# One program for the four head groups of a layer, with common buffers and the next group's first projection ahead of the last unit's turns

## The reference

```python
for l in range(DEPTH):                      # 2 layers, the context output only in the first
    h = rms_norm(x, pre_mix_g[l]) * (1 + sc1) + sh1          # x: 512 latent tokens; hc likewise: 256 context tokens
    p = split(h @ w_in[l])                                    # one input projection for four head groups
    oa = A: 4 query and 2 key/value heads of 64, RMS norm of q and k, 2-D rotary, dense
    ob = B: 4 heads of 64 + 32 (rotary), keys and values from a normed latent of 128 @ w_kv_up
    oc = C: 4 query and 2 key/value heads, keys within 128 tokens, a sink logit per head
    od = D: 4 heads, 2-D neighbourhood, a learned bias per head and offset
    # latent queries attend to their latent keys and all context keys, context queries to context keys
    x = x + g1 * rms_norm(concat(oa, ob, oc, od) @ w_out[l], post_mix_g[l])
    x = x + g2 * rms_norm(moe(h2), post_ffn_g[l])             # 64 experts, top 8, and a shared expert
# sh1, sc1, g1, sh2, sc2, g2 = split(silu(c) @ ada_w[l] + ada_b[l])
```

## Time and profile before

| stage | from to (us) | us | TensorE busy | clock |
|---|---|---|---|---|
| layer 0, A | 52.8 to 177.0 | 124.2 | 115.47 | 0.93 |
| layer 0, B | 177.0 to 317.4 | 140.4 | 126.50 | 0.96 |
| layer 0, C | 317.4 to 433.7 | 116.3 | 103.10 | 0.97 |
| layer 0, D | 433.7 to 572.7 | 139.0 | 130.82 | 1.00 |
| layer 1, A | 1645.9 to 1750.3 | 104.4 | 96.04 | 0.93 |
| layer 1, B | 1750.3 to 1873.1 | 122.8 | 108.31 | 0.93 |
| layer 1, C | 1873.1 to 1963.1 | 90.0 | 79.78 | 1.00 |
| layer 1, D | 1963.1 to 2080.5 | 117.4 | 110.71 | 1.00 |

### The profile page before, as it was taken

One profiled execution on the slowest core, in us unless ns is written; L12 is line 12 of the kernel. 1 busy time (PEld: TensorE's weight loads), 2 busy tenths in 40 slices (PEclk: granted clock), 3 DMA queues, 4 the chain that ended last, 5 costly groups with the idle time before them and its releaser, 6 DMA issues. The chain is left out here.

```text
span 2915.5 us, 44582 instructions
## 1 busy us (share of the span) xinstructions
PE 2595.9 (89%) x13635; PEld 1267.2 (43%) x13636; DVE 1081.1 (37%) x3197; ACT 588.0 (20%) x1379; POOL 390.1 (13%) x312
## 2 busy tenths in 40 slices
PE   7999989896899999999996588989978999899894
PEld 3566555543433333333332266666533333333331
DVE  3443360515333333333332643451433332233233
ACT  2323241402011111111111341331310111111111
POOL 1000001001022222221221200001010212112212
PEclk9999999997999999999998799999989999999997
DMA  7120303007478998999993402202156999998983
GB/s 275 50 91 30 130 12 132 32 13 287 169 236 301 353 327 284 324 325 334 328 367 81 188 1 90 87 34 96 37 215 235 361 397 392 389 391 297 388 313 106
DMA packets 104979, 619.27 MB, mean 212 GB/s; under 512 B 22832, under 2 KB 23088, under 8 KB 64688
## 3 DMA queue, kind: packets, MB, share of 16 engines
q1 hardware_dynamic: 71184, 530.30, 46.2%
q0 software_dynamic: 33696, 87.63, 12.3%
HBM read 578.84 MB, written 77.99 MB: 225 GB/s over the span
## 5 line engine op out<-in xcount | busy, mean ns | idle before, releaser
L1513 PE MATMUL ps<-wgu,xT 128*64 128x512 f32 x3584 | 808.0, 604 | 43.1 <-DMA wgu<-in_exp_gu 34.2
L1513 PEld LDWEIGHTS ps<-wgu,xT 128*64 128x64 f32 x3584 | 253.8, 139 | 502.2 <-issue 492.2
L1522 PE MATMUL ps<-wd,hiddenT 128*64 128x512 f32 x1824 | 420.3, 603 | 11.2 <-issue 10.8
L624 PE MATMUL ps<-w_in,hT 128*128 128x512 f32 (+5 forms) x1152 | 369.0, 479 | 14.7 <-PEq L574 3.8
L1442 POOL DMA_INDIRECT ffn_rows<-Y,six x114 | 182.6, 1602 | 1110.8 <-issue 635.3
L1695 DVE TENSOR_TENSOR hidden<-silu,ps 128x256 f32<-128x256 f32 x112 | 47.2, 421 | 704.3 <-ACT silu L1631 698.5
L624 PEld LDWEIGHTS ps<-w_in,hT 128*128 128x128 f32 x1152 | 218.0, 196 | 155.7 <-issue 136.0
L1522 PEld LDWEIGHTS ps<-wd,hiddenT 128*64 128x64 f32 x1824 | 123.2, 137 | 227.7 <-issue 227.7
L1631 ACT ACTIVATE silu<-ps 128x256 f32<-128x256 f32 x112 | 43.1, 385 | 797.7 <-PE ps L1513 797.7
L1626 ACT ACTIVATE Y<-ps,wc 128x512 f32<-128x512 f32 x114 | 78.4, 688 | 417.4 <-PE ps L1522 417.4
L1689 DVE TENSOR_SCALAR Y<-ps,wc 128x512 f32<-128x512 f32 x114 | 85.6, 751 | 198.4 <-PE ps L1522 198.4
(11 more groups left out here) (490 smaller groups left out, 2724.1 us busy)
## 6 DMA issues: line engine op xcount, KB each, us to landing
wgu<-in_exp_gu SPq DMA_DIRECT2D x128, 2048.0 KB, 22.9
wd<-in_exp_d SPq DMA_DIRECT2D x128, 1024.0 KB, 8.2
ada_start<-in_ada_w SPq DMA_DIRECT2D x8, 1024.0 KB, 8.0
w_in<-in_w_in SPq DMA_DIRECT2D x4, 2048.0 KB, 10.8
w_in<-in_w_out SPq DMA_DIRECT2D x4, 2048.0 KB, 12.4
aw_0A<-in_ada_w SPq DMA_DIRECT2D x6, 1024.0 KB, 4.8
aw_0B<-in_ada_w SPq DMA_DIRECT2D x6, 1024.0 KB, 4.8
aw_0C<-in_ada_w SPq DMA_DIRECT2D x6, 1024.0 KB, 4.8
```

What stands on the lines that cost most here:

```text
L624: last = pe.matmul(pp[i % 2][:, at:at + c1 - c0], hT[:, k, i * P:(i + 1) * P], wg[g % 2][:, k, c0:c1], start=(k == 0), stop=(k == KD - 1))
L1513: last = pe.matmul(ps[h * HB:(h + 1) * HB, 0, :], xT[:, k, h * HB:(h + 1) * HB], wgu[w[h]][:, k, :], start=(k == 0), stop=(k == KD - 1))
L1522: last = pe.matmul(ps[h * HB:(h + 1) * HB, 1 + c, :], G[:, f, h * HB:(h + 1) * HB], wd[w[h]][:, f, c * 512:(c + 1) * 512], start=(f == 0), ...
```

## The change

The mixer no longer opens a program of its own. It returns its engines' streams as functions, and `mixers` puts those of the four groups one behind the other in one program per layer, on common buffers. Inside:

- `GroupSignal` reads the signal's base and moves it on at once, so that four groups can be written into one program; a wait for a count of 0 or -1 now waits for the group before.
- `first_tile` (the weights' wait and `project(0)`) of the next group is issued in front of the last unit's `turn_probs`.
- `KT`, the work rows `T1` to `T4`, `wup`, `cn`, `cT` and the bias `TD` lie in one buffer. `TD` overlaps the work rows, so its load waits until the rows of C are done.
- The weights of group g + 1 are loaded once the projections of group g - 1 are done; half 1 of `w_out` is loaded in D after D's projections.
- The chunks belong to the last tiles (`late = NT - NC`: 0 in layer 0, 2 in layer 1). In all groups `columns` and then `chunk` are issued after `project(i + 1)` (in B after `latent_turn`) and ahead of `turn(i)`.

```diff
+class GroupSignal:
+    def __init__(self, signal, total):
+        self.sem, self.base = signal.sem, signal.base
+        signal.stage_over(total)
+    def wait(self, eng, count):
+        if self.base + count > 0:
+            eng.wait_ge(self.sem, self.base + count)
...
-                for g in range(4):
-                    mixer(env, l, g, nt, hT, wg, oT)
+                mixers(env, l, nt, hT, wg, oT)
...
+        shared = sb("KT_and_work", [P, 4 * NROW + 4 * 384 + 512 + 4 * P])
...
+        self.TD = shared[:, 2 * NROW:2 * NROW + 60 * GRID_W].rearrange("p (h r c) -> p h r c", h=4, r=15)
...
+    late = NT - NC
...
+    def sync(sp):
...
+        if isB:
+            sp.dma_start(wup[:, :], v.t["w_up"][l]).then_inc(s_extra.sem, 16)
         load_chunk(0)
         load_chunk(1)
+        s_proj.wait(sp, 0)
+        if isD:
+            s_rows.wait(sp, 0)
+            sp.dma_start(TD[:, :, :, :], v.t["bias"][l]).then_inc(s_extra.sem, 16)
         if g < 3:
             load_w_in(v, sp, l, g + 1, wg)
         else:
             load_w_out(v, sp, l, 0, wg)
         for j in range(2, NC):
             load_chunk(j)
+        if isD:
+            s_proj.wait(sp, NT)
+            load_w_out(v, sp, l, 1, wg)
...
+    def project(pe, i):
+        if i < 2:
+            s_exp.wait(pe, i - 1)
...
+    def first_tile(pe):
+        s_w.wait(pe, 16)
+        project(pe, 0)
...
-                s_w.wait(pe, 16)
-                if isB:
-                    s_wup.wait(pe, 16)
-                project(0)
-                for i in range(NT):
-                    if i + 1 < NT:
-                        project(i + 1)
-                    if isB:
-                        latent_turn(i)
-                        if i < NC:
-                            chunk(i)
-                        latent_up(i)
-                        if 0 < i <= NC:
-                            columns(i - 1)
-                    turn(i)
-                    if not isB:
-                        if 0 < i <= NC:
-                            columns(i - 1)
-                        if i < NC:
-                            chunk(i)
-                if NC == NT:
-                    columns(NC - 1)
+        if g == 0:
+            first_tile(pe)
+        if isB:
+            s_extra.wait(pe, 16)
+        for i in range(NT):
+            if i + 1 < NT:
+                project(pe, i + 1)
+            if isB:
+                latent_turn(i)
+            if i > late:
+                columns(i - late - 1)
+            if i >= late:
+                chunk(i - late)
+            if isB:
+                latent_up(i)
+            turn(i)
+        columns(NC - 1)
...
         for u in range(NU):
             if u + 1 < NU:
                 scores(u + 1)
             if u and u % 2 == 0:
                 values(u // 2 - 1)
+            if u == NU - 1 and following:
+                following.first_tile(pe)
             turn_probs(u)
         values(NU // 2 - 1)
...
+            @block.tensor
+            def _(pe):
+                for group, following in zip(groups, groups[1:] + [None]):
+                    group.tensor(pe, following)
```

More of the change, by code:

```diff
@@ L13 @@
+from collections import namedtuple
 from contextlib import ExitStack
@@ new lines, in project @@
+    def project(pe, i):
+        if i < 2:
+            s_exp.wait(pe, i - 1)
+        s_rows.wait(pe, i - 1)
+        if not isB:
+            s_v.wait(pe, i - 1)
+        a = 0 if has_q[i] else kv0
+        if isB:
+            parts = [(0, 0, B_HALF), (B_ROW, B_HALF, W)] if has_q[i] else [(B_KR, B_KR, B_HALF), (B_LAT, W - P, W)]
+        else:
+            parts = [(c0, c0, c1) for c0, c1 in ((a, min(W, 512)), (512, W)) if c1 > c0]
+        for at, c0, c1 in parts:
+            for k in range(KD):
+                last = pe.matmul(pp[i % 2][:, at:at + c1 - c0], hT[:, k, i * P:(i + 1) * P], wg[g % 2][:, k, c0:c1],
+                                 start=(k == 0), stop=(k == KD - 1))
+        last.then_inc(s_proj.sem, 1)
@@ L575, in _, with mixers @@
+    return Programs(sync, gpsimd, tensor, scalar, vector, first_tile)
+def mixers(v, l, nt, hT, wg, oT):
+    s_step = v.S("dve_step")
+    counts = []
+    with ExitStack() as scope:
+        bufs = MixerBuffers(v, l, nt, scope)
+        groups = [mixer(v, l, g, nt, hT, wg, oT, bufs) for g in range(4)]
+        with v.nc.Block() as block:
             @block.sync
             def _(sp):
[L577 to L580, removed]
@@ L582, in _ @@
-                if isB:
[L583 to L593, removed]
+                for group in groups:
+                    group.sync(sp)
@@ L595, in _ @@
             @block.gpsimd
             def _(pool):
-                if isA or isB:
-                    n = 6 if isA else 1
-                    for i in range(NT):
[L600 to L608, removed]
+                for group in groups:
+                    group.gpsimd(pool)
@@ L610, in _ @@
             @block.tensor
             def _(pe):
-                def project(i):
-                    s_rows.wait(pe, i - 1)
-                    if not isB:
[L616 to L642, removed]
-                    s_qe.wait(pe, nq[i])
-                    s_ke.wait(pe, i)
-                    for j in range(0 if has_q[i] else NQ, NQ + NK):
-                        dst, c = (tq, j) if j < NQ else (tk, j - NQ)
-                        src = R[:, i % 2, j * KP:(j + 1) * KP]
-                        last = pe.transpose(dst[0:KP, c * P:(c + 1) * P], src, v.ident)
-                    last.then_inc(s_t.sem, 1)
@@ L718, in _ @@
-                if NC == NT:
-                    columns(NC - 1)
-                s_qe.wait(pe, nq[NT])
-                s_ke.wait(pe, NT)
-                s_pad.wait(pe, 2)
-                if not isB:
-                    s_v.wait(pe, NT)
-                scores(0)
-                for u in range(NU):
-                    if u + 1 < NU:
-                        scores(u + 1)
-                    if u and u % 2 == 0:
-                        values(u // 2 - 1)
-                    turn_probs(u)
@@ L792, in _ @@
[L792 to L800 removed]
+                for group in groups:
+                    group.scalar(act)
             @block.vector
             def _(dve):
[L804 removed]
@@ L960, in mixer @@
-    if not isB:
-        s_v.stage_over(NT)
-    if isA or isB:
-        s_ms.stage_over(NT)
-        s_rstd.stage_over(NT)
-    if isB:
-        for s, k in ((s_cn, NT), (s_ct, NT), (s_ce, NT), (s_up, NT), (s_kn, NT), (s_wup, 16)):
-            s.stage_over(k)
-    if isD:
-        s_bias.stage_over(16)
-        s_band.stage_over(1)
+                step = stepper(dve, s_step, counts)
+                for group in groups:
+                    group.vector(dve, step)
+    s_step.stage_over(counts[0])
```

623 lines of the change are left out of this document (338 added, 285 removed).

## The result

The changed kernel took 2930.12 us (median of 20 runs), the kernel before 2920.68 on the same chips (20 runs): ratio 1.0033 [1.0026, 1.0040], by which it is 9.6 us slower. Its profiled execution took 2927.45, span 2925.6; that of before 2917.33, span 2915.5.

A forecast was written before the change was run, and what follows sets the result against it. TensorE, busy for 89% of the span, was taken as the bound. Part 3's loss of 17 us minus 10.1 gained made it 7 us slower: 2926 us, own range 2918 to 2932, overall range 2906 to 2931.

The forecast's parts named there:

- part 3: In C's units, GpSimd's earlier bias pass holds a VectorE addition with two SBUF inputs: 8.5 us lost per layer, 17 in all.
- parts 1 and 2: Boundaries between head groups (part 1) and order inside the loops (part 2), with w_out: together 10.1 us faster.
- the boundary A to B: Between groups A and B in both layers, early projection, slower clock counted: 3.6 us gained, bounds 0 and 6.6.
- Rival 1: In C's units, no exclusion when GpSimd is first: part 3 costs nothing, 2909 us; chance 0.30.
- B to C, C to D: Boundaries in both layers: waits for block starts and for `out` go, 5.4 us gained, bounds 3 and 6.
- the tails of C and D: Ends of C and D, new order: layer 0 gains 1.0 and loses 0.3, layer 1 gains 0.7 each.
- A's tails: Ends of group A, new order and later chunks: 1.0 us gained in layer 0, 1.6 in layer 1.
- The order in B: In B's loop, columns moved ahead of the chunk: 2.5 us lost in layer 0, 1.5 in layer 1, sum 4.0.
- TensorE's lower clock in B: Behind the new wait at B's first latent_turn, the slow clock loses 1.5 us per layer.
- w_out: Its second half is loaded in D: the 0.7 us wait in layer 1 goes, 0.4 us gained.
- Rival 2: Fills hold back B: the clock costs all that boundary A to B gave, tails give nothing; 2917 to 2918; chance 0.08.
- Rival 3: At the boundaries, the projection ahead of the last turns waits itself; no size given; chance 0.02.

The follow-up runs named there:

- run 1: The changed kernel with GpSimd's pass over D's bias held back until D's second tile is projected; 2917.01 us, ratio 0.9979.
- run 2: The changed kernel, pass left in C's units, the addition written as tensor_scalar with only one SBUF tensor input; 2915.69 us, ratio 0.9977.
- run 3: The kernel before, with one GpSimd addition over a spare tile added in C's units in each layer; 2930.74 us, ratio 1.0031.
- run 6: The changed kernel with GpSimd's pass back in D and the old order of chunk, columns and turn inside the loops; 2919.89 us, ratio 1.0000.
- run 7: The changed kernel with GpSimd's pass back in D and each group's first projection at the group's own start; 2906.69 us, ratio 0.9955.

## Why the prediction was right: point by point

The time, 2926, lies 4 us under the measured one, and its sign and cause hold. That it is so near is in part luck. The loss of part 3 was put 1.2 us too high (17 for 15.8) and the gain of parts 1 and 2 4.0 too high (10.1 for 6.1), and the two offset each other in part; inside part 1 the boundary A to B has the wrong sign. By its own steps:

**Part 3, the exclusion, was right.** Predicted: the pass at 379 to 387, one addition of 5 to 8 us in it, 8.5 us per layer, 17 in all. Shown: the pass at 380.36 to 388.66; additions of 6.67 and 5.03; 6.7 and 7.0 in D by the table, 15.8 by the ratios of run 1 and after (13.8 to 15.8 against 17). Of the 8.5 per layer 6.5 stood for TensorE's wait and 2 for the clock; shown are waits of 5.53 and 5.65, and 1.2 and 1.4 beyond them. Runs 1 and 2 take the cause away from either side, run 3 makes it on the kernel before. Rival 1 (2909, chance 0.30) falls. The section "Who interferes with whom" of the page "SBUF — State Buffer" in the Trainium skill says of two such instructions that the first to issue holds the ports for its whole length. The trace agrees, in the order that the earlier trace rows left open.

**Parts 1 and 2 together were too large:** predicted 10.1 faster; the kernel with the pass in D is 0.21% faster, 6.1 us [2.6, 9.3], with 7.7 in the mixer by the table.

- B to C, C to D and the tails of C and D: predicted 5.4 and 2.1 (1.0 and 0.7 in C, -0.3 and 0.7 in D), in sum 7.5; the table shows 7.8 (0.5, 3.6, 1.5, 2.2). The sum is right; run 6 shows that the order's share in layer 0 has the wrong sign: 2.1 lost in C and D where 0.7 gained stood.
- A's tails: predicted 2.6, the table shows 4.6, of which 1.6 in layer 0 is what A varies by.
- The order in B: predicted 4.0 lost. The wait ahead of `turn` is 0.78 (at 208.73) in place of 0.44, as foreseen, but the sum is smaller. From `latent_turn(0)` to `latent_turn(5)` run 7, which has the new order and no wait at its start, takes 1.3 and 0.2 us more than before; the last tile of layer 1, with its chunk, takes 0.9 more. That is 2.5 us; run 6 gives back 2.0.
- **The step that failed is the boundary A to B: predicted 3.6 gained, measured about 2.7 lost** (B +4.7 in two layers, less the order's 2.0). Up to `latent_turn(0)` the mechanism was right. From the first projection to `latent_turn(0)` 20.87 us are shown (171.44 to 192.31) where 20.2 was worked out, and the wait is 4.14 for 3.4. Before, that stretch was 23.5 (173.82 to 197.35; the prediction's own rows, to 197.5, give 23.7), and in layer 1 it went from 24.8 to 22.3: 5.2 gained in the two layers for 6.6.
- The term that was mis-sized is TensorE's lower clock in B, put at 1.5 per layer, 3.0 in all; shown are about 8.2. Behind the new wait, in layer 0, chunk and `latent_up` take 1.73 and 2.08 in place of 1.07 and 1.13: 1.6 us. In layer 1 `latent_up`, `turn` and the third projection take 2.08, 1.91 and 8.24 in place of 1.13, 1.05 and 7.50: 2.6. Layer 1 has another such stretch from 1807, behind a wait of 1.54 that was there before without it: 1.6.

```profile
1773.10 0.39 PE L663 MATMUL ps<-cst,KT_and_work 128*128 128x128 f32 x1 [4.15 <-DVE R L917]
1773.95 2.08 PE L668 MATMUL ps<-KT_and_work 128*128 128x512 f32 x2 [0.46 <-ACT KT_and_work L782]
1776.81 1.91 PE L679 MATMUL ps<-cst,R 128*96 128x128 f32 x8 [0.78 <-issue]
1778.51 8.24 PE L650 MATMUL ps<-w_in,hT 128*128 128x224 f32 x32
...
1807.29 1.94 PE L307 MATMUL ps<-aw,csil 128*32 128x256 f32 x16
1809.15 1.89 PE L668 MATMUL ps<-KT_and_work 128*128 128x512 f32 x2
```

- The last 2.4 us of the 8.2 are in B's last tile in layer 0. The wait there was in the kernel before (3.64 at 250.53); the lower clock behind it lasted 3 us then and past 260 now:

```profile
250.00:254.00 4.00, 3.47 (x19) 1.49 (x20) 0.35 (x2) 0.37 (x1) 0.00 (x0) 0.57 0.00 0
254.00:258.00 4.00, 2.62 (x18) 2.00 (x18) 0.85 (x2) 1.50 (x4) 0.00 (x0) 1.00 0.00 0
```

```profile
248.00:252.00 4.00, 3.55 (x22) 2.13 (x23) 0.29 (x1) 0.37 (x1) 0.00 (x0) 0.50 0.00 0
...
256.00:260.00 4.00, 3.06 (x8) 1.92 (x8) 0.87 (x2) 0.85 (x2) 0.00 (x0) 0.50 1.03 414
```

(windows of the kernel before, then of after). From `latent_turn(5)` to the scores 7.1 us became 9.5 (248.45 to 257.93). This part can't be put down to the change: in run 3, whose code here is that of the kernel before, the same stretch takes 8.8, with the clock at 0.50 past 258:

```profile
254.00:258.00 4.00, 3.06 (x9) 1.78 (x8) 0.87 (x2) 0.85 (x2) 0.00 (x0) 0.50 0.00 0
```

So the boundary gave 5.2 and lost 5.8 to the clock where the trace can hold the change to it, and 2.4 more in the last tile: 3.0 lost in all, near the 2.7 of the table. Why the clock comes back later stays open.

- `w_out`: predicted 0.4 gained. The wait for its second half, 0.67 us of TensorE's weight loads at 2088.65 before, is gone, but it had held the products up by 0.1 only: the matmul behind it takes 0.70 where 0.59 is usual.

**What I did not weigh** is the larger lesson of part 1. I compared the early projection with the kernel before, where the gap for `wup` stood at the boundary, and not with the merged program without it. In the merged program the gap is gone anyway, since `wup` is there. VectorE's 12.7 us would then have lain beside 15 us of projections; the early projection leaves it 9.3. Of the whole change, the merging with the new order and the later tiles of the chunks gives 13 us (run 7, 0.9955), the early projection takes back 7 (run 1, 0.9979) and GpSimd's pass 16.

Rival 2 (2917 to 2918) had its first half right in size, that the clock in B costs what the boundary gave and more, and its second half wrong: the tails do give. Rival 3 falls: the early projections start without a wait (171.44, 1750.84).

## What to carry to other kernels

When programs are merged, list what each in-order queue now starts earlier, down to the engine that nobody was waiting for: here a load went out 63 us sooner (371.07 after, 434.58 before), GpSimd followed it into a stretch where VectorE was on the path, and that cost more than the boundary gave. Moving work forward on the busiest engine did not pay here, because the engine that prepares its next input did not get ahead with it; count the partner's work between the two points (12.7 us here) against what will lie beside it with and without the move (9.3 or 15). And judge each edit of a change against the kernel with the other edits in place.

## What the runs showed of the hardware

- A GpSimd addition over SBUF holds a VectorE `tensor_tensor` with both inputs in SBUF until it ends: 6.67, 5.03, 6.10 and 6.10 us for one element per partition. The same sum as `tensor_scalar` with a pointer scalar takes 0.20, and `tensor_tensor` with one input in PSUM 0.29, beside the same pass.
- A GpSimd fill leaves those `tensor_tensor` alone (0.15), but a VectorE `tensor_scalar` from SBUF to SBUF of 128x128 was held for its whole 2.65 us. The same section of the Trainium skill says that `copy` and `tensor_scalar` can enter modes that use both port pairs, and that they can then contend with GpSimd; the row agrees, though none shows the mode itself. VectorE's record starts 0.03 us ahead of the fill's and it was VectorE that waited, so starts this close don't tell who was first at the ports.
- TensorE's clock was at its lower level (0.50, 1.2 GHz) behind waits of 3.6 to 5.7 us. How long it stayed there differs between executions of the same code: behind 3.64 and 3.65 us of waiting ahead of `latent_turn(5)` it was low for about 3 us in the kernel before and for about 13 in run 3 (246 to 260). In the kernel without the early projection it also fell behind a wait of 1.25 us for `apart` (360.75 in C of layer 0), which in D of the changed kernel (510.30) no fall follows.
